# Two of seven adaLN modulation blocks moved from the first attention pair to the page choice, and the samples' mLSTM keys and queries copied out of PSUM as soon as they are there

## The chip, the cores and the metric

One NeuronCore of a Trainium2 chip runs the whole step. The metric is the device time of one execution in microseconds (us). Engine names: PE is TensorE, PEld its weight loads, DVE VectorE, ACT ScalarE, POOL GpSimd, SP SyncE; a q behind a name (SPq) is that engine's own queue of waits, registers and DMA issues.

## What is computed

One decoder layer with two branches that share a combined projection, on a prompt of 512 tokens and on 8 sample rows with a paged key/value cache:

```
mod = silu(c) @ w_ada + b_ada -> (shift, scale, gate)
h   = RMSNorm(x) * (1 + scale) + shift
z   = h @ w_in      (att q,k,v,silu gate | mLSTM q,k,v,o,silu gate | i,f logits | merge gates A,B)
A   = block-sparse causal attention (8 heads x 64; samples choose 3 of 8 past blocks of 256 keys)
B   = conv + SiLU on q,k; mLSTM matrix memory (4 heads); per-head RMSNorm; sigmoid(o)
u   = sigmoid(ga) * ((A*silu(za)) @ w_att) + sigmoid(gm) * ((B*silu(zm)) @ w_mlstm)
y   = RMSNorm(x + gate * (u @ w_out))
```

All is float32. Matrix products on the large operands are made in three passes of high and low parts (hH, hL with wH, wL). The samples' part reads 8 MB of keys for each of four pairs of heads (t = 0 to 3) and 8 MB of values for each of four later stages.

## The kernel before, in words

Five instruction streams are written out by hand, and semaphores tie them. The unit of the projections is a **tile** (`ztile`, line 553): 128 columns of a weight against all 520 tokens, 96 matmuls in two halves. Around it SP loads the raw weight (`tile`, 382), ACT makes its high part (`high`, 1013), POOL its low part (`low`, 1507), PE multiplies, and ACT or DVE takes the result out of PSUM and frees the slot (`leave`, 1018). Two PSUM slots are for tiles (banks 0 to 3), banks 4 to 7 for everything else.

**Modulation.** w_ada comes in blocks of 512 columns of 2 MB (`ada_block`, 412): blocks 0 to 3 are shift and scale, which h needs; block 4 (`W_Q`) is the samples' query weight for all heads, from w_in; blocks 5 and 6 are the gate, first used near the end (the wait on `mod_rdy` before line 950). A block's product is `modulation` (587), ACT copies it (`ada_leave`, 1054), PE turns it (`mod_turn`, 595), DVE adds the bias (`bias_added`, 1721). The two buffers for blocks are the memory of the four page slots (`ada` and `page` are both columns 0 to 8191 of arenaA), so no page may be loaded over a block that is not used up: SP waits for `ada_used` 7 (line 451) before the first page.

**Attention** (`attention(t, before)` on each engine) runs over four pairs of heads, the first written out (`before` is False), the others in a hardware loop. Each has four tiles (q, k, v, gate), for each of two heads the scores (`qk`, 661), the mask and maximum on DVE (`causal_max`, 1804 to 1809), the exponentials on ACT (1134), transposes (`ptrans`, 668) and the product with v (`pv`, 674). Beside it the samples' key pages stream: SP issues 8 steps of 4 pages of 256 KB (`key_pages`, `step`, 398 and 399) in the order 0, 3, 2, 1, 4, 7, 5, 6 with two tiles at the start and one each before the third and fifth step; step s uses page slot s % 4 and waits until DVE has freed it. DVE multiplies a step by the query (1823; POOL does so for steps 3, 7 and 5, line 1553) and sums it (1827). In the first pair DVE, ACT and PE also compute the mLSTM gates (`gates_in` 1759 to 1768, `gate_logs` 1115 and 1116, `gate_sums`, `gate_max`, `gate_stabilisers`), and blocks 4, 5 and 6 are multiplied.

**Page choice**, after the last pair: DVE finishes steps 7, 6 and 5, convolves for mLSTM head 0 (1886, 1889), ranks the blocks (1915 to 1926), PE spreads the penalties (872), DVE adds them and takes maxima (1931, 1936), while tiles 4 and 5 of mLSTM head 0 run. Value pages are loaded from here on (`value_pages`): step s of the first four waits until `page_free` of its slot counts 9.

**mLSTM** over four heads (`mlstm(h, first)`): the score products (783), POOL weights the value pages (`value_step`, 1585) and DVE sums them (1964, 1969).

**Gates stage** (from T_GATE): four tiles written out, among them the samples' mLSTM work. PE transposes the samples' q and k into banks 4 and 5 (892) and multiplies the last values (900, semaphore `sam_pe` 3 and 4). ACT waits for DVE's line 2046 (`vsum_rdy`), then makes four copies of banks 4 and 5 (1362, 1363, into `kqr` and `kqN`), then its share of the next tiles. DVE makes the low part (2051), the state sums of the samples (2055 to 2064) and `yaT` (2076); ACT and POOL then split yaT (1375, 1626). PE goes on with `key_query` (923) once ACT's `sums_leave` (1256) and DVE's low part are there.

Four waits matter most: SP's before the first key page (line 451), SP's before the first value pages, PE's before the gate sums (713), and ACT's before the copies into `kqr` and `kqN`:

```
sp.wait_ge(ada_used, 7)
sp.wait_ge(page_free[s % 4], 1 + 2 * PAIRS)
pe.wait_ge(g_dve, 3)
act.wait_ge(vsum_rdy, 2 * MH)
```

## Time and profile before

| what | value |
|---|---|
| median of 3 runs | 739.0 us (738.61 to 739.69) |
| the profiled execution | 740.05 us, its span 738.3 us |
| PE busy | 688.9 us (93%) |
| DVE, ACT, POOL busy | 478.2, 333.3, 433.6 us |
| the chain of work that ended last | PE 56%, SPq 13%, DVE 12%, issue 9%, POOL 4%, DMA 4%, ACT 2% |
| HBM | 135.10 MB read, 9.11 MB written, 195 GB/s over the span |

The profile comes from one execution, which was 1 us above the median. Busy time of PE is not work at full rate, since pipelined matmuls that run at half clock count as busy too. So the stages are to be read one by one, with the granted clock (PEclk, 1.00 is 2.4 GHz, 0.50 is 1.2 GHz) beside the busy time.

### The profile page before, as it was taken

The numbers are of one execution on the slowest core, as the hardware profiler recorded it, in microseconds if no ns is written. First come the engines' busy times: TensorE is split into PE (matmuls) and PEld (weight loads), VectorE is DVE, ScalarE is ACT, GpSimd is POOL, SyncE is SP. The second block draws the span as 40 slices with busy tenths as digits, with TensorE's granted clock in tenths as the row PEclk, the third lists the DMA queues.
The fourth block names the chain that finished last, engine by engine and source line by source line (L and its number), as shares of the span: only waits on it lengthen the run. The fifth ranks groups of instructions, "written<-read, shape, count | busy, mean of one in ns | idle before, by whom it ended". The sixth has DMA issues, their size and how long they took to land.

```text
span 738.3 us, 14736 instructions
## 1 busy us (share of the span) xinstructions
PE 688.9 (93%) x5012; PEld 611.1 (83%) x5012; DVE 478.2 (65%) x483; ACT 333.3 (45%) x727; POOL 433.6 (59%) x278
## 2 busy tenths in 40 slices
PE   2899999999998979999999999999889999999996
PEld 0575888786877857999999999997789998999974
DVE  0630579898999974995697597760665349444435
ACT  5543474746364335564463545512412224332643
POOL 4210267776675617699689688751594557666520
PEclk9898899998999989999999999999899999999999
DMA  8976868888898781287867668748447356732202
GB/s 314 344 268 202 252 168 251 267 236 282 237 309 263 218 252 29 87 235 213 235 205 210 200 196 250 214 154 239 108 118 220 99 153 176 240 108 85 87 24 92
DMA packets 156904, 144.72 MB, mean 196 GB/s; under 512 B 7547, under 2 KB 115152, under 8 KB 156852
## 3 DMA queue, kind: packets, MB, share of 16 engines
q1 hardware_dynamic: 142984, 137.15, 62.0%
q10 hardware_dynamic: 13876, 7.02, 3.1%
q8 instruction: 23, 0.38, 0.2%
q14 instruction: 21, 0.17, 0.1%
HBM read 135.10 MB, written 9.11 MB: 195 GB/s over the span
## 4 chain that ended last, share of the span: by engine, by line
PE 56%; SPq 13%; DVE 12%; issue 9%; POOL 4%; DMA 4%; ACT 2%; DVEq 0%; POOLq 0%; ACTq 0%
PE ps L553 39%; SPq L398 6%; SPq L399 4%; DVE sb_arenaA L1823 3%; PE ps L983 3%; DMA sb_arenaA<-in_w_ada 3%; PE ps L822 2%; POOL sb_wL L1507 2%; POOL sb_arenaA L1585 1%; PE ps L587 1%; PE ps L783 1%; DVE sb_arenaA L1969 1%; DVE sb_arenaB L1969 1%; DVE sb_arenaA L1964 1%; DVE sb_arenaA L1827 1%
## 5 line engine op out<-in xcount | busy, mean ns | idle before, releaser
L1507 POOL TENSOR_TENSOR sb_wL<-sb_wraw,sb_wH 128x512 fp32r<-128x512 f32 (+1 forms) x168 | 224.6, 1353 | 200.4 <-ACT sb_wH L1013 185.2
L553 PE MATMUL ps<-sb_hH,sb_wH 128*128 128x260 f32 x1152 | 240.5, 290 | 2.9 <-POOL sb_wL L1507 2.0
L553 PE MATMUL ps<-sb_hL,sb_wH 128*128 128x260 f32 x1152 | 234.9, 286 | 0.0
L553 PE MATMUL ps<-sb_hH,sb_wL 128*128 128x260 f32 x1152 | 234.8, 286 | 0.0
L553 PEld LDWEIGHTS ps<-sb_hH,sb_wH 128*128 128x128 f32 x1152 | 180.8, 192 | 16.0 <-issue 11.1
L553 PEld LDWEIGHTS ps<-sb_hL,sb_wH 128*128 128x128 f32 x1152 | 180.9, 192 | 0.0
L553 PEld LDWEIGHTS ps<-sb_hH,sb_wL 128*128 128x128 f32 x1152 | 180.8, 192 | 0.0
L1013 ACT ACTIVATE sb_wH<-sb_wraw 128x512 fp32r<-128x512 f32 (+1 forms) x168 | 98.9, 612 | 180.6 <-PE ps L553 149.5
L1585 POOL TENSOR_TENSOR sb_arenaA<-sb_arenaA 128x2048 f32<-128x2048 f32 x28 | 101.5, 3627 | 1.9 <-DMA sb_arenaA<-in_cache_v 1.9
L1827 DVE TENSOR_REDUCE sb_arenaA<-sb_arenaA 128x2048 f32 (+1 forms) x32 | 72.9, 2285 | 3.2 <-DVE sb_arenaA L1823 2.5
L1553 POOL TENSOR_TENSOR sb_arenaA<-sb_arenaA 128x2048 f32<-128x2048 f32 x11 | 54.7, 4972 | 27.0 <-DMA sb_arenaA<-in_cache_k 27.0
L1823 DVE TENSOR_TENSOR sb_arenaA<-sb_arenaA 128x2048 f32<-128x2048 f32 x21 | 61.2, 2914 | 5.0 <-DMA sb_arenaA<-in_cache_k 4.8
L1964 DVE TENSOR_REDUCE sb_arenaA<-sb_arenaA 128x512 f32<-128x4096 f32 x7 | 53.6, 7653 | 0.2 <-POOL sb_arenaA L1585 0.2
L1969 DVE TENSOR_REDUCE sb_arenaA<-sb_arenaA 128x512 f32<-128x4608 f32 x4 | 34.3, 8569 | 0.0
L1969 DVE TENSOR_REDUCE sb_arenaB<-sb_arenaA 128x512 f32<-128x4608 f32 x3 | 25.6, 8543 | 13.1 <-POOL sb_arenaA L1585 13.1
L1018 ACT ACTIVATE sb_arenaB<-ps 128x520 f32<-128x520 f32 (+1 forms) x57 | 33.9, 595 | 0.1
L587 PE MATMUL ps<-sb_arenaA,sb_gated 128*32 128x512 f32 x112 | 18.9, 776 | 12.2 <-DMA sb_arenaA<-in_w_ada 12.2
L1134 ACT ACTIVATE sb_arenaB<-ps,sb_nmx 128x512 f32<-128x512 f32 (+3 forms) x32 | 16.4, 527 | 29.7 <-DVE sb_nmx L1809 29.7
L2150 DVE TENSOR_TENSOR sb_arenaB<-ps,sb_arenaB 128x520 f32 x8 | 5.6, 700 | 29.6 <-PE ps L553 29.6
L674 PE MATMUL ps<-sb_arenaB 128*64 128x512 f32 (+3 forms) x64 | 21.1, 477 | 2.7 <-ACT sb_arenaA L1159 2.7
L2084 DVE CAST sb_kqr<-sb_rowsel 8x128 fp32r (+1 forms) x8 | 5.6, 694 | 25.4 <-PE ps L923 25.0
L661 PE MATMUL ps<-sb_arenaB 64*128 64x384 f32 (+3 forms) x64 | 21.6, 482 | 0.1
(390 smaller groups left out, 970.4 us busy)
## 6 DMA issues: line engine op xcount, KB each, us to landing
sb_wraw<-in_w_in SPq DMA_DIRECT2D x64, 512.0 KB, 4.9
sb_arenaA<-in_cache_k SPq DMA_DIRECT2D x128, 256.0 KB, 3.1
sb_arenaA<-in_cache_v SPq DMA_DIRECT2D x128, 256.0 KB, 3.1
sb_arenaA<-in_w_ada SPq DMA_DIRECT2D x6, 2048.0 KB, 12.3
sb_arenaB<-in_state_C SPq DMA_DIRECT2D x8, 512.0 KB, 3.9
sb_wraw<-in_w_mlstm SPq DMA_DIRECT2D x8, 512.0 KB, 4.9
sb_wraw<-in_w_out SPq DMA_DIRECT2D x8, 512.0 KB, 3.8
sb_arenaB<-in_x_prompt SPq DMA_DIRECT2D x1, 2048.0 KB
```

Of the source, the lines that this page charges most:

```text
L398: number = sp.value_load(ptab[0:1, bass.ds(first + i, 1)], min_val=0, max_val=n_phys - 1)
L399: sp.dma_start(page[:, s % 4, i * AW:(i + 1) * AW], pages[:, bass.ds(number, 1), :].rearrange("t o n -> t (o n)")).then_inc(ld_page[s % 4] ...
L553: last = mm(ps[:, 2 * s + a, 0:HALF], w[:, s, k, :], x[:, k, a * HALF:(a + 1) * HALF], start=(k == 0 and w is wH and x is xH), stop=(k == ...
L1013: f(wH[:, j % 2, part], wraw[:, j % 4, part], ACT.Copy).then_inc(hi_done, 1)
L1018: ins = f(halves(dst), zps(j % 2), func)
L1507: tt(wL[:, j % 2, part], wraw[:, j % 4, part], wH[:, j % 2, part].bitcast(F32), ALU.subtract)\
L1553: tt(four, four, qbc[:, s // 4:s // 4 + 1, :].broadcast_to([P, STEP_PAGES, AW]), ALU.mult)\
L1585: tt(heads, heads, score[:, bass.ds((8 * h + s) * 32, 32)].unsqueeze(2).broadcast_to([P, 32, DH]), ALU.mult).then_inc(pool_mult, 1)
L1823: chain(tt(four, four, qbc[:, s // 4:s // 4 + 1, :].broadcast_to([P, STEP_PAGES, AW]), ALU.mult))
L1827: v.tensor_reduce(score[:, bass.ds((8 * t + s) * 32, 32)], page[:, s % 4, :].rearrange("p (g n) -> p g n", n=DH), AX, ALU.add)\
L1964: v.tensor_reduce(vhalf, vpairs[0], AX, ALU.add).then_inc(pair_free[0], 1)
L1969: v.tensor_reduce(vacc[e], vpairs[1], AX, ALU.add).then_inc(pair_free[1], 1)
```

## The change

1. Blocks 5 and 6 leave the first pair. SP loads block 5 once page slots 2 and 3 are free after the last key step, and block 6 once slots 0 and 1 are; tiles 2 and 3 of that stretch come behind them. The first value pages wait for the blocks' products (`ada_used` 6 or 7). PE multiplies both (bank 6) around the halves of tile 5 in the page choice, turns them after line 872, ACT copies them between its leaves, DVE adds the bias inside the choice.
2. SP waits for `ada_used` 5 instead of 7 before the first key page. Block 4 is multiplied before the gate logits instead of after tile 0.
3. In the first pair tiles are cut into halves and moved between the gate steps, the gate logits go to bank 5 earlier, and DVE takes key step 0 before `gate_sums` and key step 1 after the convolved states.
4. ACT copies banks 4 and 5 into `kqN` alone, at `sam_pe` 3, does its share of the tiles, and makes `kqr` from `kqN` after `sam_pe` 4. DVE makes the state sums before line 2046 and the low part.

SP:

```diff
             def value_pages(s, h, first):
                 if first and s < KV_SLOTS:
-                    sp.wait_ge(page_free[s % 4], 1 + 2 * PAIRS)
+                    sp.wait_ge(ada_used, 7 if s < 2 else 6)
...
-            for j in range(2, 4):
-                att_first(j)
-                ada_block(2 + j)
-            ada_block(6)
+            att_first(2)
+            ada_block(4)
+            att_first(3)
...
-            sp.wait_ge(ada_used, 7)
+            sp.wait_ge(ada_used, 5)
...
-            for j in (0, 1, 2, 3, "v0", "v1", 4, "v2", 5, "v3", 6, 7, "v4", "v5"):
+            for j in (0, 1, "b5", 2, "b6", 3, "v0", "v1", 4, "v2", 5, "v3", 6, 7, "v4", "v5"):
...
+                elif j[0] == "b":
+                    for s in range(2):
+                        sp.wait_ge(page_free[(2, 0)[j == "b6"] + s], 1 + 2 * PAIRS)
+                    ada_block(int(j[1]))
```

PE in the first pair (the loops that issue the small products are left out; they stay as they are, except that the turned gate logits go to bank 5 of PSUM instead of 6), then in the page choice, where the last score product of `mlstm(0, True)` now also waits for `mod_rdy` 5:

```diff
             ztile(1, T_ATT + 1, hH, hL, parts=(0,))
+            pe.wait_ge(h_dve, 4)
+            pe.wait_ge(mod_rdy, 4)
+            modulation(W_Q, 7)
...
-                    modulation(W_Q, 7)
-                ztile(1, n + 1, hH, hL, parts=(0, 1) if before else (1,))
...
                     pe.wait_ge(gt_ev, 1)
-                    modulation(5, 5)
...
                     last.then_inc(g_mm, 1)
-                    modulation(6, 4)
+                    ztile(1, n + 1, hH, hL, parts=(1,))
+                    pe.wait_ge(q_lo, 1)
+                pe.wait_ge(pt_ev, 2 * t + 1)
+                query_copy(0, t, 4)
...
                     last.then_inc(g_pe, 1)
-                    mod_turn(5, 1, 6, 0)
-                    mod_turn(6, 0, 6, 36)
-                    pe.wait_ge(q_lo, 1)
-                    pe.wait_ge(mod_rdy, 5)
...
                 qk(0, t)
+                ztile(2, n + 2, hH, hL, parts=(0, 1) if before else (0,))
...
-                ztile(2, n + 2, hH, hL)
+                    ztile(2, n + 2, hH, hL, parts=(1,))
...
+                    ztile(3, n + 3, hH, hL, parts=(0,))
                     pe.wait_ge(g_dve, 6)
...
-            ztile(5, T_ML + 5, hH, hL)
+            pe.wait_ge(sel_act, 1)
+            modulation(5, 6)
+            ztile(5, T_ML + 5, hH, hL, parts=(0,))
+            pe.wait_ge(ada_ev, 5)
+            modulation(6, 6)
+            ztile(5, T_ML + 5, hH, hL, parts=(1,))
...
-            pe.wait_ge(sel_act, 1)
+            pe.wait_ge(ada_ev, 6)
+            mod_turn(5, 1, 6, 0)
+            mod_turn(6, 0, 6, 36)
             mlstm(0, True)
```

ACT. In the first pair the copy of block 4 also moves ahead of `high(2)` and `gate_rows` right behind it. In the page choice and at the samples:

```diff
                 f(qkc[:, e, :], ps[:, 4 + e, :], ACT.Silu).then_inc(sg_rdy, 1)
+                if e == 0:
+                    ada_leave(5, 6, 4).then_inc(ada_ev, 1)
             high(2, T_ML + 6, T_ML // 4 + 1)
             leave(0, T_ML + 4, go[:, 0, :], ACT.Sigmoid, chunk(goS, 0))
+            ada_leave(6, 6, 4).then_inc(ada_ev, 1)
...
-            act.wait_ge(vsum_rdy, 2 * MH)
-            for dst in (kqr, kqN):
-                f(dst[:, 0:AW], ps[0:B, 4, :], ACT.Copy, scale=KSCALE)
-                last = f(dst[:, AW:2 * AW], ps[0:B, 5, :], ACT.Copy)
-            last.then_inc(sam_act, 1)
+            f(kqN[:, 0:AW], ps[0:B, 4, :], ACT.Copy, scale=KSCALE)
+            f(kqN[:, AW:2 * AW], ps[0:B, 5, :], ACT.Copy).then_inc(sam_act, 1)
             high(0, T_GATE + 4, T_GATE // 4 + 1)
             gate_leave(2, 0)
+            high(1, T_GATE + 5, T_GATE // 4 + 1)
+            gate_leave(3, 0)
+            act.wait_ge(sam_act, 3)
+            act.wait_ge(sam_pe, 4)
+            f(kqr[:, 0:2 * AW], kqN[:, :], ACT.Copy).then_inc(sam_act, 1)
             act.wait_ge(ys_mm, 1)
             sums_leave(MH, 7, P).then_inc(ys_ev, 1)
-            high(1, T_GATE + 5, T_GATE // 4 + 1)
-            gate_leave(3, 0)
```

DVE in the attention pairs; the two lines on `t_mod` come back in the page choice, behind the additions of line 1931. At the samples, lines 2046 to 2051 now stand behind the state sums (2055 to 2064), and `kqr`'s low part waits for `sam_act` 4.

```diff
                     gates_in()
+                    key_step(0, t)
                     gate_sums()
-                    dve.wait_ge(t_mod, 6)
-                    bias_added(slice(16, 24), 6, 0).then_inc(mod_rdy, 1)
...
-                key_step(0, t)
+                key_step(0 if before else 1, t)
                 causal_max(1, t)
                 key_step(3, t)
                 inverse_sums(1, t)
-                for s in (1, 2, 4):
+                for s in (1, 2, 4) if before else (2, 4):
```

## Rows read from the trace of the kernel before

**Rows 1.** Busy time by stage (us, instructions), PEclk, DMA share, GB/s

```profile
119.00:158.00 39.00, 38.10 (x265) 32.00 (x264) 35.87 (x37) 22.47 (x55) 24.25 (x9) 1.00 0.86 261
...
271.00:285.00 14.00, 12.97 (x56) 9.57 (x56) 7.93 (x9) 4.68 (x10) 2.78 (x3) 0.72 0.20 62
```

**Rows 2.** Timeline of PE, first pair (start, us, line, tiles)

```profile
46.59 0.40 PE L643 MATMUL ps<-sb_hH,sb_wif 128*16 128x256 f32 x2
...
53.33 1.92 PE L587 MATMUL ps<-sb_arenaA,sb_gated 128*32 128x512 f32 x16
...
60.93 1.18 PE L708 MATMUL ps<-sb_pairsum,sb_scr 16*128 16x8 f32 x10
63.32 3.32 PE L587 MATMUL ps<-sb_arenaA,sb_gated 128*32 128x512 f32 x16 [1.21 <-DMA sb_arenaA<-in_w_ada]
66.57 0.86 PE L715 MATMUL ps<-sb_lf,sb_upper 128*128 128x4 f32 x4
...
69.08 2.24 PE L595 MATMUL ps<-sb_groupsum,sb_gated 128*128 128x9 f32 x16
...
72.81 4.63 PE L661 MATMUL ps<-sb_arenaB 64*128 64x384 f32 x8
...
94.50 2.42 PE L661 MATMUL ps<-sb_arenaB 64*128 64x512 f32 x8
```

**Rows 3.** Timeline of ACT in the first pair

```profile
64.53 0.22 ACT L1116 ACTIVATE sb_gf<-sb_gf 128x20 f32<-128x20 f32 x1
```

**Rows 4.** SP issues; last row: one DMA's KB and us to landing

```profile
36.20 0.37 SPq L412 DMA_DIRECT2D sb_arenaA<-in_w_in  x1
...
55.31 0.37 SPq L412 DMA_DIRECT2D sb_arenaA<-in_w_ada  x1
...
69.32 9.38 SPq L399 DMA_DIRECT2D sb_arenaA<-in_cache_k  x8
...
sb_arenaA<-in_w_in SPq DMA_DIRECT2D x1, 2048.0 KB, 9.0
```

**Rows 5.** Timeline of DVE to the last key step, then one row of POOL

```profile
96.96 0.89 DVE L1804 TENSOR_TENSOR ps<-ps,sb_cmask 128x128 f32<-128x128 f32 x4 [4.51 <-PE ps L661]
...
119.18 0.88 DVE L1804 TENSOR_TENSOR ps<-ps,sb_cmask 128x128 f32<-128x128 f32 x4
...
143.14 2.29 DVE L1823 TENSOR_TENSOR sb_arenaA<-sb_arenaA 128x2048 f32<-128x2048 f32 x1 [1.97 <-DMA sb_arenaA<-in_cache_k]
...
162.91 5.49 DVE L1823 TENSOR_TENSOR sb_arenaA<-sb_arenaA 128x2048 f32<-128x2048 f32 x1
...
253.69 2.29 DVE L1827 TENSOR_REDUCE sb_arenaA<-sb_arenaA 128x32 f32<-128x2048 f32 x1
...
161.63 4.62 POOL L1553 TENSOR_TENSOR sb_arenaA<-sb_arenaA 128x2048 f32<-128x2048 f32 x1
```

**Rows 6.** Timeline of PE and POOL in the page choice

```profile
257.72 1.91 PE L867 MATMUL ps<-sb_arenaA,sb_colsel 128*8 128x128 f32 x16
...
269.46 2.07 PE L872 MATMUL ps<-sb_scr,sb_ones 8*128 8x512 f32 x2 [3.89 <-DVE sb_scr L1926]
271.46 4.32 PE L783 MATMUL ps<-sb_arenaB 128*128 128x512 f32 x8
...
285.30 3.63 POOL L1585 TENSOR_TENSOR sb_arenaA<-sb_arenaA 128x2048 f32<-128x2048 f32 x1
```

**Rows 7.** Timeline of the samples' work: PE, then ACT, DVE, POOL

```profile
521.91 2.04 PE L923 MATMUL ps<-sb_kqr 8*128 8x512 f32 x4 [2.07 <-ACT sb_yaS L1256]
...
540.58 0.51 PE L553 MATMUL ps<-sb_hH,sb_wH 128*128 128x260 f32 x2 [2.00 <-POOL sb_wL L1507]
...
517.90 0.59 ACT L1362 ACTIVATE sb_kqr<-ps 8x512 fp32r<-8x512 f32 x1 [15.04 <-DVE sb_arenaB L2046]
...
519.95 1.21 DVE L2051 TENSOR_TENSOR sb_kqr<-sb_kqN,sb_kqr 8x1024 fp32r<-8x1024 f32 x1 [1.91 <-ACT sb_kqN L1363]
...
532.77 4.68 POOL L1626 TENSOR_TENSOR sb_yaL<-sb_gated,sb_yaH 128x2080 fp32r<-128x2080 f32 x1 [5.43 <-ACT sb_yaH L1375]
```

48 lines of the change are left out of this document (25 added, 23 removed).

## The prediction, before the changed kernel was seen

> **What bounds the kernel now.** I read the busy time by stage first, then the timeline of each engine around the three places that the diff touches. PE is busy nearly everywhere, so a stage counts only where PE is idle, slow, or itself held by another stream. Three such places exist. In the first attention pair PE runs small products and blocks 5 and 6 at half clock: the same head's score products take 4.63 us at 72.81 and 2.42 us at 94.50 [rows 2]. In the pairs after it DVE and SP set the pace: from 119 to 158 us DVE works 35.9 of 39 us, and PE 38.1, so PE has hardly any slack either [rows 1]. SP issues 8 pages in 9.38 us, 1.17 us a page, so a pair's 32 pages cost it at least 37.5 us plus four tiles, and at 143.14 DVE waits 1.97 us for pages [rows 4, 5]. In the samples' stage PE waits 2.07 us for ACT and later 2.00 us for POOL, and between them the clock falls (a key_query group takes 2.04 us) [rows 7]. All times below are on the clock of the old run unless I say new.
>
> **First pair on PE, walked anew.** Block 4 is issued at 36.20 and takes 9.0 us, so it is there at 45.2; PE reaches it at 46.59, where the gate logits began, so it costs its own 1.92 us and no wait [rows 2, 4]. What stood between 46.59 and 53.33 (6.7 us) follows, ending at 55.2. The query product (0.7), ACT's copy of the gate rows (it ends at 56.4 behind one high part) and the turned logits (1.18) end at 57.7. These logits ended at 62.1 before (60.93 + 1.18). Tile 1's second half (3.1) covers the logs to 60.8. From the logits' end to the logs took 2.65 us before (64.53 + 0.22 - 62.1) [rows 3]; ACT now has four short copies (1.5 us) in front and is done at 61.3. The query copy (1.1) ends near 61.9, the gate sums take 2.5 us (66.57 to 69.08) to 64.4. The score products begin there instead of at 72.81: 8.4 us earlier. What went is block 5's product (about 1.9), block 6's (3.32 and 1.21 of waiting) and both turns (2.24) [rows 2]. At full clock the products end at 66.9 instead of 77.44, 10.5 us earlier. The rest of the first pair is PE work in the same amount; some 0.5 us comes from tile 2, which began at half clock. So head two's products end 11 us earlier, and DVE's row at 96.96 moves to 86. If the half clock stays, as it did after 1.21 us of idleness and the small products of 60.93 and 66.57, 2.2 us of this is lost on the products and about 1.2 on the tile. The new stretch has no idle piece over 0.6 us, so I take the full clock, and keep 3.4 us for the bound.
>
> **First pair on DVE and SP.** SP may issue the first page at about 50 instead of 69.32, since it waits for block 4 only. Step 0 is there by 58, and DVE takes it (4.6 us) at about 63, once the query is copied, while it used to wait; step 1 goes where step 0 stood. Both lie in time in which DVE waits for PE, up to 86. So the DVE chain from head two's mask to the next pair is one step shorter, 4.5 us. That next pair began at 119.18, 22.2 us after 96.96. From 86 DVE would be there at 103.7, but PE's products of the next pair, which are moved by 11 us and had 1.9 us of slack, come at 106.4 [rows 5]. SP is held too: step 7 needs the slot of step 3, freed only at 91, so SP loses again most of its 19 us. From 91 it issues steps 7, 5, 6 and the next pair's first four with two pairs of tiles, about 35 us, and is at step 4 at 127 where it was at 141.7. That gives 14.7 us for SP, 15 for DVE without its page waits, 11.5 to 12.7 for PE, whose 0.9 us of slack per pair is small. The three then run together. I take **14 us** at the last key step, 253.69 [rows 5]. The bounds are 9 (half clock, and PE in front throughout: 11 - 3.4 + 1.5) and 17 (DVE's full 11 + 4.5 and the waits for pages).
>
> One row speaks against the moved steps: DVE's product at 162.91 took 5.49 instead of 2.29 us while POOL's ran from 161.63 for 4.62 us [rows 5]. Step 0's product now meets POOL's low parts of tile 3, 2.5 us at most; DVE has that until the masks are due. The Trainium skill (SBUF — State Buffer, "Who interferes with whom") says that a DVE instruction with two SBUF inputs and a GpSimd one that reads SBUF take turns, each blocked for the whole of the other. By that rule the trace agrees, and a step that falls on a POOL key step would cost 4.6 us, which the lower bound already holds.
>
> **Page choice.** Block 5 needs slots 2 and 3, free about 4.6 us before the last key step ends; block 6 needs that end, 256.0 (253.69 + 2.29) [rows 5]. A block alone took 8.0 us (issued 55.31, used at 63.32) [rows 2, 4]. Block 5 so lands at 259.5 to 261. Block 6 queues behind its rest and tile 2, and lands at 265 to 268. PE ends the column sums at 259.63 (257.72 + 1.91), takes block 5 at 260.3, tile 5's half until 265.1, block 6 at 266.3, the other half until 271.1. The penalty product was ready at 269.46 [rows 6]. Then the turns (2.24) go ahead of the score products. That is 1.6 + 2.2 = 3.8 us more. Against it, PE had idled 3.89 us before 269.46 and ran at 0.72 until 285 [rows 1, 6]: the penalties took 2.07 and the score products 4.32 us, 1.0 and 2.2 more than at full clock. Without the long idle piece PE likely keeps the clock and gives back 3.2 us here and some on tile 6. DVE's bias (0.25) and reduction then end about 1.5 us late. I take **+1.5 us**; bounds -1 and +6 (the clock falls nonetheless, block 6 as late as 268).
>
> The value pages wait for block 6's product, so step 0 is issued from 268 and is there at 275; POOL takes it at 285.30 [rows 6]. The other three follow at 279, 285 and 289, ahead of their uses at 291, 295 and 298. Ten microseconds cover this; without them each microsecond would count. The Trainium skill (DMA: Bandwidth & Descriptors, "Queues, rings and completion order") says that each DMA engine consumes a ring's descriptors in order. By it block 5 would not be slowed by block 6 behind it, as I assumed; by sharing instead it would land 2 to 3 us later, inside the bound. No run here shows which.
>
> **Samples.** ACT waited 15.04 us for line 2046 before its copies at 517.90 [rows 7]. Now kqN is there at 508.5, the state sums run on DVE before 517 with nothing waiting behind them, and ACT's high and leave work of tiles 4 and 5 is done by 516.3. After the last values (517.0) one copy from SBUF replaces four; no row has its form, so I bound it by 0.6 and 1.2 us and take 1.0. The low part (1.21 at 519.95) ends at 519.4, PE's page sums and their copy at 520.0. So key_query starts 1.8 us before 521.91, and faster by 0.9 if the clock holds. DVE's yaT is ready at 521 instead of 530.5, since the 8.5 us of state sums are gone from there; ACT (1.94) and POOL (4.68 at 532.77) end at 528 instead of 537.4. The low part behind which PE waited 2.00 us at 540.58 is early. With the waits go the slow matmuls: 2.0 us in the two tiles after 523.9, 1.6 in the two after 540.6. Sum: 1.8 + 0.9 + 2.0 + 2.0 + 1.6 = 8.3. PE still idles 0.9 us at 517, so I take **7.5**; bounds 4 (only waits, clock low as before) and 9.
>
> **Sum.** -14 + 1.5 - 7.5 = -20.0 us. Span 738.3 to 718.3, the profiled execution 740.05 to 720.05. That execution was 1.05 us above the median of 739.0, so the median becomes **719.0 us**. After the choice and after the samples PE is busy without breaks, so nothing swallows a shift there.
>
> **Rivals.**
> 1. *PE holds the attention.* PE's 38.1 of 39 us [rows 1] and a clock that stays low in the first pair leave only 9 to 11 us there: -10 + 1.5 - 7.5 gives 723. For: the half clock of 63.32 to 80 came after similar small products. Against: there is dense tile work until 60.8.
> 2. *The choice pays.* Clock low and block 6 late cost 6: 723.5. For: the stage's clock was 0.72. Against: its idle piece is cut up.
> 3. *More than the sum*, all three at their good ends, 17 + 1 + 9: 712.
> 4. *Not what it says*: DVE and SP are bound by page transport, so the earlier start only lengthens SP's wait for slots; the first two terms cancel to -2, the samples bring little: 734 to 738.
> 5. *Slower*: block 6 becomes the bound of the choice. It holds PE's tile 5, the last score product and all value pages. Measured from 256, it would have to be used 20 us later than 268 for the stage to eat the other 21.5 us; then step 0 would land at 295, ten behind POOL, and PE would restart at 1.2 GHz: about 741. Against: alone a block took 8 us.
>
> **Chances.** Forecast 0.62; rival 1 0.13; rival 2 0.09; rival 3 0.08; rival 4 0.05; rival 5 0.03. Range 712.5 to 727. Within 0.2% (1.5 us, about what this measurement can tell) I put 0.02, from rival 4's end; faster 0.95, slower 0.03.
>
> **What the changed profile would show.** First page issue near 50; scores of head one near 64.5 and 2.4 us long; the last key step ending near 242; two blocks landing within 16 us of that, PE's clock above 0.9 after them; no 15 us wait of ACT at the samples; no POOL wait of PE behind key_query. The forecast is wrong if PE waits over 2 us for block 6, if the next pair starts later than 20 us after head two's mask, or if key_query still takes 2.0 us.

## The result, and the profile after

| what | before | after |
|---|---|---|
| median (lowest to highest) on one chip, 9 runs each | 738.61 us (735.39 to 743.98) | 731.77 us (727.48 to 737.73) |
| ratio of the two | | 0.9894, 95% interval 0.9863 to 0.9925 |
| the same kernel again later, on another chip | 738.96 us, 19 runs | 730.02 us, 12 runs; ratio 0.9894 (0.9863 to 0.9925) |
| the profiled execution, its span | 740.05, 738.3 us | 734.37, 731.4 us |

The change makes the kernel 1.1% faster: 7 to 9 us, where 20 were forecast. Medians in this document are over all executions of a row, ratios leave out those that are over 1.5% above the fastest of their kernel, and the profiles of a2_after, c2_fill_samples and c3_fill_choice are of such slow executions, so no time rests on one of these three alone. Executions of either kernel lie up to 10 us apart, and their time goes with the mean granted clock: of the nine of the changed kernel the shortest had a mean clock of 0.977 (727.48 us), the longest 0.959 (737.73 us). A single profile is therefore read beside those of the experiments.

The page of the profile after: span, busy time, and the chain of work that ended last.

```profile
span 731.4 us, 14741 instructions
...
PE 685.4 (94%) x5012; PEld 611.4 (84%) x5012; DVE 470.9 (64%) x483; ACT 334.2 (46%) x726; POOL 429.9 (59%) x278
...
PE 59%; SPq 12%; DVE 10%; issue 7%; POOL 5%; DMA 5%; ACT 1%; ACTq 0%; DVEq 0%; POOLq 0%
```

PE is busy 3.5 us less and still holds nearly the whole span. The next view is the busy time by stage. Its columns: window, length, then PE, PEld, DVE, ACT and POOL with their instructions, granted clock, DMA share, GB/s.

```profile
46.00:63.00 17.00, 17.00 (x134) 13.05 (x133) 5.54 (x12) 12.11 (x25) 4.16 (x4) 1.00 0.65 190
63.00:74.00 11.00, 11.00 (x43) 8.48 (x43) 6.59 (x13) 3.52 (x10) 3.65 (x2) 0.53 0.86 262
...
158.00:200.00 42.00, 38.79 (x256) 32.63 (x255) 38.83 (x35) 22.64 (x56) 27.33 (x12) 0.96 0.86 256
...
263.00:281.00 18.00, 16.97 (x90) 13.21 (x89) 8.09 (x10) 5.90 (x14) 2.78 (x3) 0.81 0.85 250
...
516.00:533.00 17.00, 16.27 (x102) 15.36 (x103) 6.35 (x12) 4.70 (x7) 12.91 (x6) 0.80 0.28 71
...
610.00:628.00 18.00, 16.26 (x124) 15.97 (x123) 14.53 (x17) 6.57 (x14) 13.43 (x13) 0.91 0.55 150
```

From 46 us on, besides short pieces in pairs three and four (0.96 from 158 to 200), four stretches are not at full clock. From 63 to 74 it is 0.53, though the trace, whose matmul ends are modelled, has PE busy in every microsecond from 46 to 74. In the choice it is 0.81 (0.72 in [rows 1]), at the samples 0.80, and once late, at 610 to 628, where the kernel before had 1.00.

**First attention pair.** Timeline of PE after the change:

```profile
62.75 0.84 PE L723 MATMUL ps<-sb_lf,sb_ones 128*128 128x4 f32 x6
63.53 4.63 PE L667 MATMUL ps<-sb_arenaB 64*128 64x384 f32 x8
...
86.91 2.42 PE L667 MATMUL ps<-sb_arenaB 64*128 64x512 f32 x8 [0.35 <-ACT sb_arenaB L1155]
```

The score products of head one start at 63.53 instead of 72.81 [rows 2]: 9.3 us earlier, 0.9 more than forecast. But they still take 4.63 us. Head two's start at 86.91 instead of 94.50, a gain of only 7.6: from one to the other takes 23.4 us instead of 21.7. In this stretch the clock comes back 9.9 us after head one's products start (7.8 before), and PE waits 0.50 and 0.35 us for ACT. Timelines of DVE and SP:

```profile
89.37 0.89 DVE L1814 TENSOR_TENSOR ps<-ps,sb_cmask 128x128 f32<-128x128 f32 x4 [5.16 <-PE ps L667]
...
92.10 2.27 DVE L1837 TENSOR_REDUCE sb_arenaA<-sb_arenaA 128x32 f32<-128x2048 f32 x1
...
107.49 0.69 DVE L1850 TENSOR_TENSOR sb_gated<-sb_gated,ps 128x512 f32<-128x512 f32 x1 [3.00 <-PE ps L680]
109.77 0.89 DVE L1814 TENSOR_TENSOR ps<-ps,sb_cmask 128x128 f32<-128x128 f32 x4 [1.60 <-PE ps L667]
```

```profile
51.38 9.48 SPq L399 DMA_DIRECT2D sb_arenaA<-in_cache_k  x8
...
72.50 36.30 SPq L399 DMA_DIRECT2D sb_arenaA<-in_cache_k  x16
109.53 1.08 SPq L382 DMA_DIRECT2D sb_wraw<-in_w_in  x2
```

DVE waits 5.16 us for head two's products, and at the end of the pair waits for PE again, 3.00 and 1.60 us. From head two's mask to the next pair's it takes 20.4 us instead of 22.2 (96.96 to 119.18 [rows 5]), so the key step that was moved ahead, 4.5 us, gives 1.8 of them: PE comes last. SP issues its first page at 51.38 instead of 69.32 [rows 4], 17.9 us earlier, but its third group of 16 pages takes 36.30 us, because step 7 needs slot three, which DVE frees with the sum at 92.10, behind head two's mask. Its next tiles go out at 109.53; before, they went out at 117.47, so 7.9 us of the 17.9 are left. The later pairs, first SP and DVE of the kernel before, then PE and DVE of the changed one:

```profile
117.47 1.07 SPq L382 DMA_DIRECT2D sb_wraw<-in_w_in  x2
...
157.69 0.89 DVE L1804 TENSOR_TENSOR ps<-ps,sb_cmask 128x128 f32<-128x128 f32 x4
...
199.10 0.89 DVE L1804 TENSOR_TENSOR ps<-ps,sb_cmask 128x128 f32<-128x128 f32 x4
...
225.46 2.29 DVE L1823 TENSOR_TENSOR sb_arenaA<-sb_arenaA 128x2048 f32<-128x2048 f32 x1 [1.17 <-DMA sb_arenaA<-in_cache_k]
```

```profile
175.42 1.85 PE L674 MATMUL ps<-sb_ident,sb_arenaB 128*128 128x128 f32 x10 [2.76 <-ACT sb_arenaB L1148]
...
217.72 2.39 PE L674 MATMUL ps<-sb_ident,sb_arenaB 128*128 128x128 f32 x10 [3.34 <-ACT sb_arenaB L1148]
```

```profile
148.24 0.89 DVE L1814 TENSOR_TENSOR ps<-ps,sb_cmask 128x128 f32<-128x128 f32 x4
...
175.43 2.29 DVE L1833 TENSOR_TENSOR sb_arenaA<-sb_arenaA 128x2048 f32<-128x2048 f32 x1 [2.02 <-DMA sb_arenaA<-in_cache_k]
...
189.99 0.88 DVE L1814 TENSOR_TENSOR ps<-ps,sb_cmask 128x128 f32<-128x128 f32 x4
...
219.06 2.63 DVE L1833 TENSOR_TENSOR sb_arenaA<-sb_arenaA 128x2048 f32<-128x2048 f32 x1 [3.33 <-DMA sb_arenaA<-in_cache_k]
...
246.18 2.29 DVE L1837 TENSOR_REDUCE sb_arenaA<-sb_arenaA 128x32 f32<-128x2048 f32 x1
```

Head one's masks of pairs two, three and four stand at 109.77, 148.24 and 189.99; before they stood at 119.18 [rows 5], 157.69 and 199.10. The distances are nearly the same, 38.5 and 41.75 us after the change, 38.5 and 41.4 before. So the lead is 9.4, 9.4 and 9.1 us at these masks, and the last key step ends at 248.47 instead of 255.98: 7.5 us. The last 1.6 us go in pair four, where DVE waits 3.33 us for a page instead of 1.17.

**Page choice.** PE, then DVE:

```profile
252.06 1.92 PE L590 MATMUL ps<-sb_arenaA,sb_gated 128*32 128x512 f32 x16
...
259.92 1.92 PE L590 MATMUL ps<-sb_arenaA,sb_gated 128*32 128x512 f32 x16 [2.87 <-DMA sb_arenaA<-in_w_ada]
...
264.85 1.12 PE L877 MATMUL ps<-sb_scr,sb_ones 8*128 8x512 f32 x2
...
267.70 4.09 PE L783 MATMUL ps<-sb_arenaB 128*128 128x512 f32 x8
...
285.34 4.58 PE L822 MATMUL ps<-sb_arenaB 128*128 128x257 f32 x20
```

```profile
261.53 0.68 DVE L1935 TENSOR_TENSOR sb_scr<-sb_pen,sb_ident 8x512 f32<-8x512 f32 x1
266.00 1.28 DVE L1940 TENSOR_TENSOR sb_arenaA<-sb_arenaA,ps 128x512 f32<-128x512 f32 x2 [3.80 <-PE ps L877]
```

Block five is there in time. PE waits 2.87 us for block six, then runs half a tile, and only then the penalty product, although DVE had its operand at 262.2 and now waits 3.80 us. From the last key step to the first value product (line 822) it takes 36.9 us, against 33.3 before (that product stood at 289.33): the choice costs 3.5 us. PE is at full clock through its wait and until 267.7, so the penalty product takes 1.12 us instead of 2.07; the score products behind the turns are at half clock for most of their 4.09 us.

**Samples.** PE, ACT and DVE:

```profile
513.91 1.02 PE L573 MATMUL ps<-sb_ones,sb_arenaA 128*128 128x1 f32 x8 [0.90 <-DVE sb_arenaB L2073]
...
516.73 1.50 PE L930 MATMUL ps<-sb_kqr 8*128 8x512 f32 x4 [0.90 <-DVE sb_kqr L2078]
...
532.56 1.19 PE L930 MATMUL ps<-sb_kqr 8*128 8x512 f32 x4
```

```profile
503.41 0.59 ACT L1370 ACTIVATE sb_kqN<-ps 8x512 f32<-8x512 f32 x1 [4.58 <-PE ps L899]
...
513.13 1.06 ACT L1378 ACTIVATE sb_kqr<-sb_kqN 8x1024 fp32r<-8x1024 f32 x1 [0.47 <-PE ps L907]
```

```profile
505.12 0.67 DVE L2061 TENSOR_TENSOR sb_qsN<-sb_qsN,sb_aw 8x512 f32<-8x512 f32 x1
...
515.06 1.21 DVE L2078 TENSOR_TENSOR sb_kqr<-sb_kqN,sb_kqr 8x1024 fp32r<-8x1024 f32 x1
```

ACT's wait of 15.04 us [rows 7] is gone, the state sums take 0.67 to 0.68 us each, and PE no longer waits for POOL behind the second key_query. Yet the clock still falls: key_query takes 1.50 us and the two tiles behind it end at 532.56, 14.3 us later, where the third gap takes 11.6. The third key_query product starts at 545.39 instead of 553.81.

### The profile page after: what moved, and what is told of

Its sections match the earlier page's. It is cut to its first block, busy times and chain, and to the rows that moved or that the text cites. A ratio compares the mean times of both kernels' runs of the same rounds, so it can differ in the third digit from the quotient of the medians.

```text
span 731.4 us, 14741 instructions
## 1 busy us (share of the span) xinstructions
PE 685.4 (94%) x5012; PEld 611.4 (84%) x5012; DVE 470.9 (64%) x483; ACT 334.2 (46%) x726; POOL 429.9 (59%) x278
## 4 chain that ended last, share of the span: by engine, by line
PE 59%; SPq 12%; DVE 10%; issue 7%; POOL 5%; DMA 5%; ACT 1%; ACTq 0%; DVEq 0%; POOLq 0%
PE ps L556 42%; SPq L398 5%; SPq L399 4%; DMA sb_arenaA<-in_w_ada 3%; PE ps L990 3%; PE ps L822 2%; DVE sb_arenaA L1833 2%; POOL sb_arenaA L1563 2%; POOL sb_arenaA L1595 2%; POOL sb_wL L1517 2%; PE ps L930 1%; PE ps L590 1%; DVE sb_arenaA L1980 1%; DVE sb_arenaB L1980 1%; PE ps L783 1%
## 5 line engine op out<-in xcount | busy, mean ns | idle before, releaser
L1517 POOL TENSOR_TENSOR sb_wL<-sb_wraw,sb_wH 128x512 fp32r<-128x512 f32 (+1 forms) x168 | 222.3, 1338 | 202.0 <-ACT sb_wH L1020 183.6
L1833 DVE TENSOR_TENSOR sb_arenaA<-sb_arenaA 128x2048 f32<-128x2048 f32 x21 | 59.1, 2816 | 7.3 <-DMA sb_arenaA<-in_cache_k 6.3
L590 PE MATMUL ps<-sb_arenaA,sb_gated 128*32 128x512 f32 x112 | 16.7, 722 | 15.6 <-DMA sb_arenaA<-in_w_ada 15.6
L1141 ACT ACTIVATE sb_arenaB<-ps,sb_nmx 128x512 f32<-128x512 f32 (+3 forms) x32 | 16.4, 526 | 29.3 <-DVE sb_nmx L1819 29.3
L590 PEld LDWEIGHTS ps<-sb_arenaA,sb_gated 128*32 128x32 f32 x112 | 3.6, 123 | 22.1 <-issue 21.4
```

What stands on the lines that cost most here:

```text
L1517: tt(wL[:, j % 2, part], wraw[:, j % 4, part], wH[:, j % 2, part].bitcast(F32), ALU.subtract)\
L1833: chain(tt(four, four, qbc[:, s // 4:s // 4 + 1, :].broadcast_to([P, STEP_PAGES, AW]), ALU.mult))
```

## The experiments

Sixteen kernels ran, in four groups, each with runs of the kernel before on the same chip. This table holds what the median and the profile of each say. "Keys" is the end of the last key step, "choice" the time from there to the first value product (line 822 of the changed kernel), "samples" that from the second head's first value product to the third key_query product, "rest" what follows that to the end of the span.

| kernel | median us | ratio (95%) | keys | choice | samples | rest |
|---|---|---|---|---|---|---|
| before | 738.61 | | 255.98 | 33.3 | 207.4 | 184.5 |
| after | 731.77 | 0.9894 (0.9863 to 0.9925) | 248.47 | 36.9 | 203.0 | 186.0 |
| a2_after | 730.02 | 0.9894 (0.9863 to 0.9925) | 250.98 | 39.3 | 202.8 | 186.1 |
| e1_samples | 732.19 | 0.9916 (0.9882 to 0.9949) | 254.10 | 33.1 | 201.2 | 184.5 |
| e2_blocks | 736.63 | 0.9918 (0.9882 to 0.9954) | 246.92 | 37.6 | 207.3 | 186.0 |
| e3_noblocks | 727.27 | 0.9816 (0.9772 to 0.9859) | 245.74 | 33.2 | 202.8 | 186.0 |
| e4_oldkeys | 732.08 | 0.9897 (0.9852 to 0.9943) | 247.09 | 35.8 | 203.6 | 184.5 |
| e5_latepages | 732.24 | 0.9887 (0.9842 to 0.9932) | 248.04 | 36.3 | 202.9 | 184.5 |
| c1_fill_first | 731.10 | 0.9873 (0.9831 to 0.9915) | 248.76 | 36.9 | 202.8 | 184.5 |
| c2_fill_samples | 726.67 | 0.9793 (0.9739 to 0.9847) | 247.89 | 39.4 | 203.7 | 186.1 |
| c3_fill_choice | 734.27 | 0.9903 (0.9857 to 0.9950) | 252.75 | 40.9 | 203.0 | 186.0 |
| c4_fixedpages | 725.77 | 0.9787 (0.9734 to 0.9841) | 242.47 | 35.9 | 202.8 | 186.1 |
| d1_batch | 733.57 | 0.9892 (0.9852 to 0.9933) | 247.47 | 36.7 | 203.0 | 184.6 |
| d2_batch_fill | 730.20 | 0.9855 (0.9795 to 0.9915) | 247.58 | 36.6 | 201.3 | 184.5 |
| d3_samples_fill | 733.77 | 0.9923 (0.9888 to 0.9957) | 256.01 | 35.2 | 200.7 | 184.5 |
| g1_tile | 730.88 | 0.9897 (0.9860 to 0.9935) | 246.20 | 35.9 | 203.1 | 184.5 |
| g2_step3 | 730.10 | 0.9897 (0.9862 to 0.9931) | 245.84 | 37.2 | 201.5 | 184.5 |
| g3_both_fill | 723.13 | 0.9809 (0.9771 to 0.9847) | 246.01 | 35.3 | 202.1 | 184.5 |

**Each half alone.** e1_samples is the kernel before with the samples part alone, e2_blocks the changed kernel with the old samples part:

```
-            act.wait_ge(vsum_rdy, 2 * MH)
-            for dst in (kqr, kqN):
-                f(dst[:, 0:AW], ps[0:B, 4, :], ACT.Copy, scale=KSCALE)
-                last = f(dst[:, AW:2 * AW], ps[0:B, 5, :], ACT.Copy)
...
+            f(kqN[:, 0:AW], ps[0:B, 4, :], ACT.Copy, scale=KSCALE)
+            f(kqN[:, AW:2 * AW], ps[0:B, 5, :], ACT.Copy).then_inc(sam_act, 1)
...
```

> The kernel before with the samples' part alone (ACT copies kqN at once, makes kqr later, DVE's order). Theory A (the clock: PE is at half clock behind the wait of the samples, as in the changed kernel, where two tiles took 14.4 us instead of 11.5): key_query starts about 1.2 us early, POOL's 2 us wait goes, 4 to 4.5 us in all, median 734 to 735. Theory B (the page's own figures without a clock loss, as I forecast): 7.5 us, median 731. If the two parts of the change act on each other, it is neither.

> The changed kernel with the samples' part taken back: only the blocks, the early pages and the key steps. Theory A (attention held by PE and its half clock, choice made longer): last key step 7.5 us earlier than before, first mLSTM value product 4 us earlier, and 4 us stay, median 734.5. Theory B (my forecast): 12.5 us, median 726. The parts add up if this and the samples' run give together the 6.8 us of the whole.

Medians 732.19 and 736.63. Either half is 0.8% by itself, both together 1.1%, within intervals 0.3 to 0.4% to each side: too wide to tell whether the halves add up. The profiles are sharper. "Samples" is 207.3 us wherever the old part stands (before, e2_blocks) and 201 to 204 wherever the new one does. "Keys" is 254 to 256 with the old block places (before, e1_samples, d3_samples_fill, mean 255.4). It is 245.7 to 248.8, mean 247.1, in the eleven profiles with the new places that count here (all but c4, which is another matter, and the three named above). So one term is 7 to 9 us and the other 4 to 6, and neither is what was forecast (14 and 7.5).

**What block loads and key step are worth.** e3_noblocks leaves blocks five and six out (their modulation is set to one, so that part of the output gate isn't computed). e4_oldkeys puts the key steps of the first pair back; e5_latepages does that and also holds the first page until the gate rows are through.

The first lines are of e3, the next of e4 and e5, the last two of e5.

```
-                    ada_block(int(j[1]))
-            modulation(5, 6)
-            modulation(6, 6)
-            mod_turn(5, 1, 6, 0)
-            mod_turn(6, 0, 6, 36)
...
-                    key_step(0, t)
-                key_step(0 if before else 1, t)
+                key_step(0, t)
...
-            sp.wait_ge(ada_used, 5)
+            sp.wait_ge(g_dve, 3)
```

> The changed kernel without modulation blocks 5 and 6: neither loaded nor multiplied nor turned, the gate is set to 1, and the first value pages wait for the page slots only. It prices the blocks in the page choice. Theory A: work of 5.7 us and a wait of 2.9 us go from PE, but PE then idles for the penalties and keeps half clock as before: 3.5 us faster than the changed kernel, 728. Theory B: the blocks lie in time in which PE idles, 1.5 us, 730. If value pages or block 6 hold anything behind the choice, more than 5 us.

> The changed kernel with the key steps of the first pair where they stood (step 0 after the convolved states, steps 1, 2 and 4 after head two's mask); pages still early. Theory A (PE holds the attention): DVE waited 3.0 and 1.6 us for PE before the next pair, the step of 4.5 us fills just that, so the time is that of the changed kernel within 1 us, 732. Theory B (DVE and SP hold it, as I forecast): 4.5 us slower, 736.

> The changed kernel with the key steps of the first pair where they stood and the first page held until the gate rows are through (about 60 instead of 51 us), so that SP gains only some 9 us there. If early pages are worth nothing because SP then waits for slot three (my reading of the trace), the pair-to-pair times and the last key step's end (247 to 248.5) stay, and the median is that of the kernel with the old order alone (732). If early pages matter, the masks of the later pairs come 2 to 9 us later and the median is 734 to 738.

Without the blocks the choice takes 33.2 us, as in the kernel before (33.3) and e1_samples (33.1); with them it takes 35.8 to 37.6 in the kernels of this stage's own order. That prices them at some 2.5 to 4.5 us, with a scatter that d3_samples_fill shows: 35.2 without the blocks there. With the old key steps DVE is 3.2 us later at pair two's mask (113.00 against 109.77), of which 1.4 stood already at head two's products (88.31 against 86.91), and nothing of it is left at the last key step (247.09). With the first page 11.6 us later as well, that step ends at 248.04:

```profile
84.31 24.13 SPq L399 DMA_DIRECT2D sb_arenaA<-in_cache_k  x16
...
111.21 10.02 SPq L399 DMA_DIRECT2D sb_arenaA<-in_cache_k  x8
```

SP's 16 issues now take 24.13 us instead of 36.30, and it is 0.3 us ahead of the changed kernel at the next group of pages (111.21 against 111.54). So the moved key step and the first 11.6 us of the early pages were worth nothing at the last key step that these profiles can tell (they scatter by 3 us), and the medians, 732.08 and 732.24 us, agree. What is left to explain the 7.5 us is that PE's products come earlier; no run takes that alone back.

**Clock.** c1, c2 and c3 add matrix products whose results nobody reads, in places where PE runs small products or waits.

```
+  def fill(bank, col, slot, count):
+      for i in range(count):
+          mm(ps[:, bank, col:col + HALF], wH[:, slot, i % 4, :], hH[:, i % 4, 0:HALF], start=True, stop=True)
```

In c1 `fill` makes 4 of them ahead of the gate sums and 12 between them, in c2 7 ahead of the page sums at the samples, 7 between and 6 behind them, in c3 22 while PE waits for block six.

> The changed kernel with 16 more matmul pairs of a tile's own form (4 before and 12 between the gate sums of the first pair), written to a free PSUM bank and never read. Theory A (the clock fell because PE had little to do from 60.5 to 63.5 us): the fillers cost 1 to 2 us, the score products of head one then take 2.4 us instead of 4.6 and tile 2 runs at full clock, head two's mask comes 2 us earlier than 89.4, and what is gained goes on to the end of the attention: 730. Theory C (attention is paced by SP's issue of pages from the slot that key step 3 frees): the same, since that slot follows head two's mask. If the clock falls with the fillers too, it does not hang on this gap, and the kernel is 1 to 2 us slower.

> The changed kernel with fillers in the samples' wait (7 before the page sums, one between each, 6 behind). Theory A: PE's clock stays at 1.00, key_query takes 1.1 instead of 1.5 us and the two tiles behind it 11.6 instead of 14.4; 3 us faster, 729. If the fall has another cause, no gain, 732.

> The changed kernel with 22 fillers while PE waits 2.9 us for block 6 in the page choice. Theory A: the score products of mLSTM head 0 take 2.2 instead of 4.1 us and tile 6 5.8 instead of 7.5: the stage up to the first value product 2 to 3.5 us shorter, 729. If not, the wait for block 6 is not what drops the clock: 732.

c1: from 63 to 74 the clock is 0.69 instead of 0.53. The score products begin 1.8 us later (65.30), take 3.51 us, and pair two's mask stands at 109.95 instead of 109.77. What the clock gave back, the added products had cost.

c3: the score products still took 4.61 us, and neither its median nor its ratio (0.9903) shows a gain. So it is not the wait for block six that drops the clock there (g1_tile, below, says the same). c2's profiled execution fell to half clock behind key_query too (0.50 from 521 to 526, with PE busy in all of 512 to 526), but its three others had a mean clock of 0.981 to 0.986 and its ratio is 0.9793. d2_batch_fill (below) shows the case in which the clock holds. Its window from 516 to 533:

```profile
516.00:533.00 17.00, 17.00 (x131) 15.80 (x130) 7.86 (x14) 5.64 (x8) 13.36 (x7) 1.00 0.34 93
```

There key_query takes 1.19 us, and from the first to the third it takes 25.7 us instead of 28.7. Taken over these two profiles, the added products cost 1.3 of the 3.0 us (from the second head's value product to key_query: 175.7 against 174.4), so "samples" falls by 1.7.

**SP's issue.** c4_fixedpages takes key pages 0 to 127 instead of the pages of the table (so the samples' attention is computed from other keys), which leaves out 128 reads of page numbers. d1_batch reads the four numbers of a step ahead of its four transfers. d2_batch_fill is d1 with c2's products, d3_samples_fill is e1 with them.

```
-                for i in range(STEP_PAGES):
-                    number = sp.value_load(ptab[0:1, bass.ds(first + i, 1)], min_val=0, max_val=n_phys - 1)
+                numbers = [sp.value_load(ptab[0:1, bass.ds(first + i, 1)], min_val=0, max_val=n_phys - 1)
+                           for i in range(STEP_PAGES)]
+                for i, number in enumerate(numbers):
```

This is d1; in c4 `number` is `first + i` for the key pages.

> The changed kernel with key pages 0 to 127 in order instead of the page table's: SP loads no page number for them (0.4 to 0.5 us less per page; same bytes, another choice of pages, so the samples' outputs change). Theory C (SP's issue paces pairs two to four at 42 us each): 32 pages save 13 us of SP per pair, so DVE becomes the bound with 37 to 39 us, each pair is 3 to 4 us shorter, 10 us in all, 722. Theory A alone (PE holds the attention): nothing, PE has 38 of 42 us of work, at most 1 to 2 us. Theory D (the DMA engines' rate holds it): nothing either, and the pages' landing times grow.

> The changed kernel with the four page numbers of a step read one after the other ahead of the step's four transfers (before, each number was read between two transfers). Output unchanged. Theory C (SP's issue of pages with their table reads paces attention pairs 2 to 4, about 1.0 to 1.1 us a page): if the read's latency or the switch between reads and issues is the cost, 8 pages take under 8 us instead of 8.5 to 10, the last key step ends 2 to 5 us earlier than in the changed kernel (248.5) and the median falls to 727 to 730. Theory D (the issue itself or the landing costs, in whatever order the reads stand): no difference, 731 to 732. If a late first transfer of a step costs more than the order gives, 733.

> The same with the extra matrix products in PE's waits of the samples' stage besides (their results are never read). If the page order and the clock at the samples are each worth what the single runs suggest (some 3 us and 3 to 5 us), 723 to 726; if the order is worth nothing, 726 to 728, as the extra products alone gave (726.7).

> The kernel before with the samples part and the extra products in the samples' waits, blocks five and six left where they stood. If moving the blocks is worth the 3 to 4 us that the changed kernel's profile shows up to the first value product, this is 3 to 4 us slower than the changed kernel with the extra products (726.7): 730. If the moved blocks are worth nothing (theory N: this kernel's samples part alone had 732.2, as much as both together), 727.

```profile
119.71 4.25 SPq L400 DMA_DIRECT2D sb_arenaA<-in_cache_k  x8
...
127.55 16.79 SPq L400 DMA_DIRECT2D sb_arenaA<-in_cache_k  x16
...
159.48 4.25 SPq L400 DMA_DIRECT2D sb_arenaA<-in_cache_k  x8
```

With fixed pages 8 issues take 4.25 us (0.53 each) where they took 8.5 to 10, and SP waits 52.5 us for slots that DVE frees between 130 and 232 us, where in the changed kernel it waits for none. A page takes longer from issue to landing (median 3.9 us instead of 3.1), so it is not the transport that got faster. DVE waits for no page at all (in the changed kernel 6.3 us between 119 and 248). Pair four's mask stands 38.8 us after pair three's instead of 41.75 (pair three's 39.8 after pair two's instead of 38.5), and the last key step ends at 242.47, 6.0 us earlier. This is the one edit to the changed kernel that moved that point by more than the scatter. Reading the numbers in fours did not do it. SP's groups of 8 are shown with 7 us, but the reads now lie ahead of them, and the period of a pair is 41.6 and 40.5 us; the median is that of the changed kernel. My expectation of 727 to 730 failed: in this order the reads cost as much. d3 against e1 (0.9923, 0.9916) shows no gain from the added products without the moved blocks. With them c2 does (0.9793, of three executions); d2 (0.9855, 0.9795 to 0.9915) overlaps d1 and the changed kernel and shows none by itself. I can't say why.

**Three aimed repairs.** g1_tile runs both halves of tile 5 before block six's product. g2_step3 takes step 3 of the first pair before the next pair's tile on POOL and before step 1 and the mask on DVE. g3_both_fill has both, and c2's products. a2_after is the changed kernel, unaltered.

```
-            ztile(5, T_ML + 5, hH, hL, parts=(0,))
+            ztile(5, T_ML + 5, hH, hL)
             pe.wait_ge(ada_ev, 5)
             modulation(6, 6)
-            ztile(5, T_ML + 5, hH, hL, parts=(1,))
...
+                if not before:
+                    key_step(3, t)
                 key_step(0 if before else 1, t)
                 causal_max(1, t)
-                key_step(3, t)
+                if before:
+                    key_step(3, t)
```

> The changed kernel with both halves of tile 5 ahead of block six's product, so that PE has 2.9 us of work while the block is under way, and the penalty product stands right behind the block. Theory B (the choice pays 3 to 3.5 us because the penalty product queues behind block six and half a tile; DVE waited 3.80 us for it): penalties start 14 us after the last key step instead of 16.4, the first value product 34 to 35 us after it instead of 36.9, median 2 to 3 us below the changed kernel. Rival (the stage is set by the half clock of the score products, or by ACT and DVE behind them): the penalties come earlier, the first value product does not, median the same.

> The changed kernel with step 3 of the first pair taken by POOL before the next pair's tile and by DVE before step 1 and head two's mask, so that slot three is free at about 82 instead of 94.4 us. Theory C (SP's pages pace attention from there on, and the early pages were worth nothing because SP then waited for that slot): SP's 16 issues that took 36.3 us take 23 to 25, its next tiles are issued 8 to 12 us earlier, and the last key step ends 3 to 6 us earlier than 248.5, median 726 to 729. Rival P (PE's own 38 to 40 us a pair set the pace, with SP only following): SP is early, the masks of the later pairs and the last key step stay within 1.5 us, median 731 to 732.

> Both of these with the extra matrix products in PE's waits at the samples. If each term holds by itself: -2.5 (choice), -4 (pages), -1.7 (clock at the samples), 723 to 725. If only the choice and the samples count, 727 to 728.

> The changed kernel again, unaltered, on the same chip as the three above: 731 to 733, with the first value product 36 to 37.5 us after the last key step and the third key_query product 203 us behind the second head's value product. Theory of chance (single profiles differ by 2 to 4 us before the samples): the last key step ends anywhere from 247 to 252.

```profile
257.59 1.92 PE L590 MATMUL ps<-sb_arenaA,sb_gated 128*32 128x512 f32 x16
260.06 1.12 PE L876 MATMUL ps<-sb_scr,sb_ones 8*128 8x512 f32 x2 [0.54 <-DVE sb_scr L1934]
261.11 2.86 PE L598 MATMUL ps<-sb_groupsum,sb_gated 128*128 128x9 f32 x16
263.82 4.62 PE L783 MATMUL ps<-sb_arenaB 128*128 128x512 f32 x8
```

In g1 block six is used without a wait, and the penalty product starts 13.9 us after the last key step instead of 16.4: 2.5 us, as expected. But the clock is then down (0.50 from 262 to 268; turns 2.86 instead of 1.95 us, score products 4.62 instead of 4.09), and the first value product gains 1.0. Both views were half right. The only time in which PE is not busy from 250 to 262 is 0.54 us, so here too the clock fell with hardly a pause.

```profile
104.27 1.08 SPq L382 DMA_DIRECT2D sb_wraw<-in_w_in  x2
106.28 13.32 SPq L399 DMA_DIRECT2D sb_arenaA<-in_cache_k  x8
...
131.68 17.98 SPq L399 DMA_DIRECT2D sb_arenaA<-in_cache_k  x16
```

In g2 SP's 16 issues take 31.63 us and its next tiles go out at 104.27, 5.3 us earlier. The group behind them then takes 13.32 instead of 8.76 us, and at 131.68 SP is 0.6 us ahead of the changed kernel (132.24). The slots are full, so there is nowhere to put a lead. From there to 173.27 it issues without a pause, 41.6 us for a pair. The last key step ends at 245.84, as in e3_noblocks, which has nothing of this edit. The lead is not worth anything that these runs can tell.

g3_both_fill has the lowest median of the versions that compute everything: 723.13 us, ratio 0.9809 (0.9771 to 0.9847), which lies clear of the changed kernel's 0.9863 to 0.9925. But c2_fill_samples, with the added products alone, has 0.9793 (0.9739 to 0.9847), so no run shows that the two repairs add to them. Its executions had a mean clock of 0.970 to 0.982. It is 7 to 9 us below the changed kernel's two medians; how they divide is not settled. In its profile the choice gave 1.6 us against the changed kernel's, the samples 0.9.

## Why the prediction was wrong

The forecast was 719.0 us, range 712.5 to 727; 731.77 lies above it, between rivals 1 and 4. The direction (faster, 0.95) was right. In the profiles: attention -7.5 where -14 stood, choice +3.5 where +1.5 stood, samples -4.4 where -7.5 stood. Sum -8.4; a half-clock piece at 616 gave 1.5 us back (the rest takes 184.5 or 186.0 us in kernels with the same code there, so I take it for chance), which leaves 6.9 at the end of the span. Two of the three signs of being wrong stood: PE waits 2.87 us for block six, and the next pair starts 20.4 us after head two's mask.

1. *The walk along PE to the score products* held: 8.4 us forecast, 9.3 measured. Its sentence that blocks 5 and 6 ran at half clock before was right for block 6 only; until 63 us the clock was 1.00.
2. *"At full clock the products end at 66.9"* failed. I kept the full clock because the new stretch has no idle piece over 0.6 us. It has none, the trace has PE busy in all of 46 to 74, and the clock is at half from about 63.4 to 73.4, behind the query copy and twenty gate sums of four columns each. Head two's products gained 7.6 us where 11 were forecast: the 3.4 us that I had put into the bound, though its sum met this by luck, since the start was 0.9 us better and the slow stretch 1.7 us longer than before. The first row of PE above is the last of these sums. So no pause that the trace shows stands before the fall; that it comes from what PE computes there is likely and not shown (with sixteen larger products in between, c1, it came some 3 us later).
3. *"So the DVE chain from head two's mask to the next pair is one step shorter, 4.5 us"* is true of DVE and was worth 1.8 us at the next pair, since DVE then waits 3.00 and 1.60 us for PE, and nothing that can be seen at the last key step (e4 and e5 end the same without it).
4. *"That gives 14.7 us for SP"* failed: the group of pages that it meant went out at 132.24 instead of 141.69, 9.5 us earlier. It rested on SP's early start and on its gain being kept. SP lost 10 of its 17.9 us at slot three, as foreseen, and has a lead only as long as four slots have room (e5 had its first page 11.6 us later, g2 its tiles at 104.27 5.3 us earlier, and both were where the changed kernel was one group or one pair on). From pair two to pair four it issues practically without a pause in both kernels, 41 to 43 us a pair (tiles at 109.53, 150.88 and 192.91; before at 117.47, 160.32 and 201.91), and c4, with issues at half the price, is the run in which this point moved. DVE's waits for pages stayed (6.3 us; 4.8 before), PE waits behind them for ACT's exponentials (2.76 at 175.42, 3.34 at 217.72), and behind each of these two waits the clock falls. In the forecast's own terms: the next pair was to start at 106.4 and started at 109.77, which is the 3.4 us of step 2, and from there the lead was to grow from 12.8 to 14 us and shrank from 9.4 to 7.5. I had this row, "1.17 us a page", and used it as the reason why SP would be earlier, not as the pace. The lower bound of 9, "PE in front throughout", was nearest and still too high.
5. *The choice's price* was mis-sized, 3.5 us for 1.5. Block six was used 11.4 us after the last key step's end (10.3 forecast). Of the 3.2 us from a held clock 1.0 came (the penalty product takes 1.12 us instead of 2.07); the 2.2 did not, 4.09 us for the score products. The part I didn't see is that the penalty product sits behind block six and half a tile on PE's queue while DVE waits 3.80 us (g1 shows 2.5 us of it). In e5_latepages the score products did take 2.40 us, and the choice still 36.3.
6. *One assumption on transfers* held. Block five was in use at 252.06, 8.1 us after its issue at 243.95, though block six and a tile were issued at 248.53 and 248.94 behind it, and block six was in use 7.9 us after that. Taking turns would have held up the first by the second. So by the rule of the Trainium skill (DMA: Bandwidth & Descriptors, "Queues, rings and completion order") that a ring's descriptors are consumed in order, the trace agrees.
7. *The samples' waits* went as told (ACT's 15.04 us, POOL's 2.00 us), and four of the five state sums even fell from 1.7 to 0.7 us. key_query started 1.2 us earlier where 1.8 stood, and from the second key_query product to the third the 3.6 us (2.0 and 1.6) came in full. *"Faster by 0.9 if the clock holds"* and the 2.0 us behind it failed: PE waits twice, 0.90 us each, with the page sums' one-column products between, and the clock falls at about 517. From the first to the second key_query product 2.9 us were to be gained and 0.35 were lost (15.83 us instead of 15.48). The low clock cost 3.0 us, nearly the whole difference between 7.5 and 4.4 (d2, where it holds: 25.7 instead of 28.7 us).

Three of the misses are one: at each of the three places I took the clock to be held because I had cut the idle pieces, and at each it was low for part of the stage. The Trainium skill (TensorE: Matmul & The Clock Gate, "HAM oscillation — how this bites in real kernels") ties the fall to waits between groups of matmuls. By that rule the trace agrees in pairs three and four (waits of 2.76 and 3.34 us). It does not at 63.53, where no wait stands, nor in g1's page choice, where PE waits 0.54 us; at the samples there are two waits of 0.90 us, and c2's clock fell there with none. The measurement decides.

Of the rivals, the first ("PE holds the attention" and its clock stays low) named the mechanism of the first pair, at 723 us; what holds the pairs after it is SP's issue (c4), not PE. The fourth ("the earlier start only lengthens SP's wait for slots") was right that most of SP's early start is lost, wrong that transport is the limit, and too dark on the rest. What they had together, 10 us in place of 14 and the choice at 4 to 6, I had priced only one at a time. The misses were not independent: a clock that stays low costs in all three terms at once, and the range should have held that sum (-9 + 6 - 4 = -7, so 732 us).

## What to carry to other kernels

A queue that issues nearly without pause sets the pace of the loop: an early start in front of it is kept only up to the number of its buffers, so price such a start by its lead one round later, not by the first issue. When a step is put on a queue in front of a late transfer, look up what small product stands behind it and who waits for that. Where the clock was low before and the new order still consists of small products and short waits, forecast it low in all places together, and let the range hold that sum.

## What had not been expected of the hardware

- The granted clock fell to half with no idle microsecond of PE in the trace, behind small products: 0.53 from 63 to 74 us (0.69 with sixteen larger products in between). In g1_tile it was 0.50 from 262 to 268, behind 12 us in which PE was idle for 0.54.
- A page issue with its page number read from memory takes SP 1.1 us, one with a fixed number 0.53 us; reading four numbers first did not shorten a pair.
- DVE's products on 8 partitions took 0.67 to 0.68 us at the samples, where four of them had taken 1.65 to 1.75 while POOL was busy; moving them in time, to where POOL is idle, made them 1 us shorter each. The fifth, a reduction with one input, took 0.67 in both.
- The same attention code stood 3 us apart in two profiles (keys at 245.74 in e3_noblocks and 248.47 in the changed kernel), and a piece late in the kernel took 184.5 or 186.0 us: either in the profiles with the new block places, 184.5 in all three with the old.
